# Modulation weights streamed under attention, interleaved projection, and 34 expert units for 35 in a two-layer hybrid block

## The chip, the cores and the metric

One core of one Trainium2 chip. The metric is the device time of the whole program in microseconds (us), the median of several runs; everything is in float32. The core has a matrix engine (TensorE, PE in the rows; PEld is its weight load), VectorE (DVE), ScalarE (ACT), GpSimd (POOL) and an engine that issues DMA transfers (SP). Each engine runs its own program in order and waits for the others by semaphores.

## The reference

Two layers of a hybrid block over 384 tokens of width 1024: tokens 0 to 127 are context (tile t = 0, condition c_ctx), tokens 128 to 383 are samples (tiles 1 and 2, condition c). Each layer computes

```
sh1, sc1, g1, sh2, sc2, g2 = split(cond @ w_mod + b_mod, 6)          # w_mod 1024 x 6144
h = rms_norm(x, g_pre_mix) * (1 + sc1) + sh1
u = h @ w_in                                                         # 1024 x 2816
y_a = silu(layer_norm(dwconv31(u_a1 * sigmoid(u_a2))))               # 256 columns
y_b = hyena(dwconv3(u_b))            # two long convolutions by spectra, gates x1, x2
y_c = rms_norm((softmax(q1 k1) - lam * softmax(q2 k2)) @ v)          # 4 heads; samples also see 128 cached keys
x = x + g1 * rms_norm(concat(y_a, y_b, y_c) @ w_out, g_post_mix)
h = rms_norm(x, g_pre_ffn) * (1 + sc2) + sh2
s = sigmoid(h @ router_w); 4 of 8 groups, then 8 of 64 experts per token
y = swiglu(h, shared) + sum over the 8 experts of weight * swiglu(h, expert e)   # width 256
x = x + g2 * rms_norm(y, g_post_ffn)
```

The outputs are x after both layers and the new keys and values of the context tokens.

## The kernel before

**Weights.** All big weights stream from DRAM by SP's DMAs. The mixer's go through RING, three slots of 4096 columns: per layer 20 chunks (`chunk`, lines 347 to 367) in a fixed order, twelve of w_mod (2 MB each), three and three of w_in, two of w_out; chunk i goes into slot i mod 3 once the chunk three places earlier has been used. The experts use four buffers (two in RING, two in WB); `free` holds a load back until the buffer's owner has been multiplied.

**Mixer, layer by layer, one stage after the other.** Modulation: `mod_chunk` (L552) multiplies a chunk with the two conditions, 16 matmuls; two chunks make a section (one of sh1, sc1, ...), whose row is turned into columns by `mod_columns` (L536). All six sections of a layer are made ahead of everything else, and in between lie the Hyena filters (L847) and their spectra (L570, L574). `gate_rows` (L584, evicted by `grow`, L1034) spreads the gates g1 and g2 over partitions, and `to_features` (L600) transposes the normalised tokens to HT. The projection runs 19 tiles u (L873 feature-major for the conformer and Hyena parts, L883 token-major for q, k, v). Then come the layer norm and the Hyena turns (z transposes, spectra and convolutions, L918 to L943) and the q and k transposes; then attention, 12 units (tile, head) in a software pipeline of 14 iterations (scores L957, transposes L967, values L979, output turns L987); then the output projection w_out (L997) for all three tiles, residual (L1271, L1273), squares (L1045), normalising, transposes, router (L1010), token rows for the gathers (L1017).

**Experts.** Experts are sorted by their token count, and each rank in that order has a fixed width. `parts(u)` makes units: pairs (96 + 32 or 64 + 64 tokens) and single experts of 128. 35 units run in the order WIDE. A unit is one `step` of TensorE: gate and up matmuls (L617) with the next unit's gathered rows transposed in between (L659), the token list of the unit three later (`lists`, L644 or L647: three float32 matmuls of three or two columns), the scatter of the unit before (L671, L672), a flip (L633) and the down matmuls (L626). POOL gathers the token rows and makes the scatter matrices. Tokens beyond a rank's width go to a loop over all 64 experts (`turns`), whose number of rounds is computed on the chip.

Of the kernel before, what the change touches and what calls it, by code (L numbers as in the profile page):

```python
# [47 lines left out]
NCH = NMOD + 3 + 3 + 2  # L48
# [4 lines left out]
NPAIR, NFULL = 29, 6  # L53
NU = NPAIR + NFULL
LSTN, SORTN = 4, 8
# [46 lines left out]
def build(nc, I, O):  # L102
    lam_init = [0.8 - 0.6 * math.exp(-0.3 * l) for l in range(DEPTH)]
    with ExitStack() as ctx:
# [18 lines left out]
        MODC = sb("MODC", [P, 6, KD, 2])  # L123
        ASC = sb("ASC", [P, 2, KD, 2])
# [4 lines left out]
        RSM = sb("RSM", [P, 200])  # L129
        NRD = sb("NRD", [P, DEPTH], mybir.dt.int32)  # L130
        h_rows = nc.dram_tensor("h_rows", [TOK, DM], F32, kind="Internal").ap()
        PASSED = sb("PASSED", [1, 32])

        with ExitStack() as mx:
# [7 lines left out]
            KS = sb("KS", [P, NT, 2, 2, 256], c=mx)  # L142
# [3 lines left out]
            YS = sb("YS", [P, NT, 2, 256], c=mx)  # L146
            ON = sb("ON", [P, 2, P], c=mx)

        with ExitStack() as me:
# [11 lines left out]
            ONEHOT = sb("ONEHOT", [P, 2, NT, P], c=me)  # L161
# [7 lines left out]
            WS = sb("WS", [P, NT, NU, 3], c=me)  # L169
# [28 lines left out]
        PS = [ctx.enter_context(nc.psum_tensor(f"PS{i}", [P, 512], F32)) for i in range(8)]  # L198
# [12 lines left out]

        FLT = QKV[:, :, :].rearrange("p a b -> p (a b)")
# [10 lines left out]
        MROW = HTF[:, 0:2048].rearrange("p (b n) -> p b n", b=2)  # L223
# [5 lines left out]
        M2 = RWF[:, 1280:1792].rearrange("p (a n) -> p a n", a=2)  # L229

        RP = YT[:, 4:8, :].rearrange("p a b -> p (a b)")
        XN = YT[:, :, :].rearrange("p a b -> p (a b)").rearrange("p (t d) -> p t d", t=NT)
        XNK = XN.rearrange("p t (q k) -> p t k q", k=KD)
# [13 lines left out]
        WIDE = (29, 30) + tuple(range(0, 5)) + (31,) + tuple(range(10, 16)) + (32,) + tuple(range(5, 10)) + (33,) + tuple(  # L247
            range(16, 22)) + (34,) + tuple(range(22, 29))
# [23 lines left out]
        chunk_in = [sem(f"chunk_in{i}") for i in range(SLOTS)]  # L272
# [23 lines left out]
        def turns(eng, l):  # L296

            rounds = eng.value_load(NRD[0:1, l:l + 1], min_val=0, max_val=NT)
            if l == 0:
# [9 lines left out]
         a_yss, a_rt, a_tk) = map(sem, (  # L309
             "a_hid", "a_mod", "a_spec", "a_cond", "a_lam", "a_grow", "a_ss", "a_hT", "a_u", "a_zt", "a_ln", "a_qk",  # L310
             "a_exp", "a_PT", "a_oss", "a_OT", "a_yss", "a_rt", "a_tk"))
# [10 lines left out]
        K_FILT, K_MOD, K_AU, K_DU, K_CV, K_SC, K_ROPE, K_LN, K_ZS, K_GATE, K_P = (  # L322
            12, 7, 23, 4, 64, 36, 48, 12, 24, 8, 48)

        def chunk_no(l, i):

            return len(range(i % SLOTS, NCH, SLOTS)) * l + i // SLOTS + 1

        def au(n):

            return {1: 1, 3: 2}[n] if n < 4 else 2 + 2 * (n - 3) if n < 10 else 14 + n - 9
# [14 lines left out]
        def _(sp):  # L346
# [37 lines left out]
            for l in range(DEPTH):  # L384
# [10 lines left out]
                for i in range(SLOTS, NCH):  # L395
                    chunk(l, i)
# [1386 lines left out]
```

## Time and profile before

| | us |
|---|---|
| three runs | 1999.53, 1992.54, 1999.26 |
| median | 1999.26 |
| the profiled execution | 2000.44 |
| its span in the trace | 1998.4 |
| TensorE busy (8604 matmuls) | 1814.4, 91% |
| VectorE, ScalarE, GpSimd busy | 634.9, 377.1, 186.1 |
| DMA | 542.05 MB, mean 271 GB/s |
| mean granted TensorE clock | 0.938 |

Times in the rows are counted from the span's start. The span lies inside the execution; 2.0 us are around it. Layer 0 fills the first half of the span, layer 1 the second. A busy share is an average over stages with different limits, so the rows of the stages say more than this table. The granted clock is a share of full speed (1.0 is 2.4 GHz, 0.5 is 1.2 GHz).

### The profile page before, as it was taken

What the parts mean: (1) busy time and instruction counts of PE and PEld (TensorE: products, weight loads), DVE (VectorE), ACT (ScalarE), POOL (GpSimd) and SP (SyncE); (2) the same over time, 40 slices, a digit from 0 to 9 for tenths busy, and PEclk for the clock granted to TensorE, in tenths of its full rate; (3) what the DMA queues carried; (4) which work ended last, traced back from release to release, by engine and by line L of the source; (5) the groups of instructions that cost most, each with busy time, mean ns of one, the idle gap of its engine ahead of it and who ended that gap; (6) DMA issues with size and microseconds to landing.
All of it is one profiled execution on the core that took longest, in us unless ns stands there. A gap on an engine that the chain in (4) does not pass through costs nothing. (4 is left out here: it accounts for less than half of the span.)

```text
span 1998.4 us, 22439 instructions
## 1 busy us (share of the span) xinstructions
PE 1814.4 (91%) x8604; PEld 896.5 (45%) x8604; DVE 634.9 (32%) x1719; ACT 377.1 (19%) x832; POOL 186.1 (9%) x181
## 2 busy tenths in 40 slices
PE   5899768689999999999888996687899999999995
PEld 1454544544444444444335545335444444444442
DVE  2255461512222222222241835605122222222222
ACT  2210241301111111111222102403111111111111
POOL 0000000011111111111000000100111111111110
PEclk8899968899999999999969998698899999999998
DMA  9723000287999999999584320002789999999992
GB/s 404 321 85 126 11 1 0 95 328 295 415 392 418 393 411 390 419 393 415 232 359 189 127 95 0 1 28 82 321 343 414 392 419 393 404 399 416 395 416 112
DMA packets 77435, 542.05 MB, mean 271 GB/s; under 512 B 8336, under 2 KB 11408, under 8 KB 21776
## 3 DMA queue, kind: packets, MB, share of 16 engines
q1 hardware_dynamic: 67248, 503.90, 61.8%
q0 software_dynamic: 10080, 36.70, 4.6%
q8 instruction: 70, 1.15, 0.2%
q14 instruction: 37, 0.30, 0.0%
HBM read 534.80 MB, written 5.77 MB: 270 GB/s over the span
## 5 line engine op out<-in xcount | busy, mean ns | idle before, releaser
L617 PE MATMUL PS<-RING,EX 128*32 128x512 f32 (+2 forms) x1280 | 387.3, 598 | 1.7 <-DVE EX L1424 1.7
L617 PE MATMUL PS<-WB,EX 128*32 128x512 f32 (+2 forms) x1408 | 387.5, 598 | 0.0
L626 PE MATMUL PS<-RING,AT 128*32 128x512 f32 (+2 forms) x688 | 220.5, 611 | 4.3 <-ACT AT L1077 3.2
L1442 DVE TENSOR_TENSOR YL<-PS,YH 128x512 fp32r<-128x512 f32 x140 | 96.9, 692 | 368.8 <-ACT YH L1093 347.2
L626 PE MATMUL PS<-WB,AT 128*32 128x512 f32 (+2 forms) x704 | 189.0, 596 | 0.0
L671 PE MATMUL PS<-YH,SCAT 128*128 128x512 f32 x420 | 177.2, 422 | 2.9 <-DVE YL L1442 2.9
L466 POOL TENSOR_SCALAR SCAT<-CST,LSTT 128x384 fp32r<-128x384 f32 x70 | 87.7, 1252 | 897.0 <-PE PS L672 885.9
L617 PEld LDWEIGHTS PS<-WB,EX 128*32 128x32 f32 (+2 forms) x1408 | 103.0, 126 | 144.1 <-issue 144.1
L672 PE MATMUL PS<-YL,SCAT 128*128 128x512 f32 x420 | 166.1, 395 | 0.0
L617 PEld LDWEIGHTS PS<-RING,EX 128*32 128x32 f32 (+2 forms) x1280 | 102.8, 128 | 119.0 <-issue 119.0
L1424 DVE COPY EX<-PS 128x512 f32<-128x512 f32 x70 | 48.4, 692 | 329.1 <-PE PS L659 329.1
L1093 ACT ACTIVATE YH<-PS 128x512 fp32r<-128x512 f32 x140 | 83.7, 598 | 249.0 <-PE PS L626 249.0
L883 PE MATMUL PS<-RING,HT 128*128 128x512 f32 x288 | 123.9, 592 | 0.0
L659 PEld LDWEIGHTS PS<-CST,XG 128*128 128x128 f32 x560 | 61.7, 142 | 107.9 <-issue 107.9
L873 PE MATMUL PS<-HT,RING 128*128 128x384 f32 x320 | 103.7, 486 | 1.5 <-ACT HT L1051 1.5
L626 PEld LDWEIGHTS PS<-RING,AT 128*32 128x32 f32 (+2 forms) x688 | 64.2, 138 | 80.1 <-issue 78.4
L552 PE MATMUL PS<-RING,COND 128*32 128x512 f32 x384 | 60.0, 754 | 36.0 <-DMA RING<-in_wmod 32.6
L659 PE MATMUL PS<-CST,XG 128*128 128x128 f32 x560 | 91.2, 286 | 0.0
L452 POOL TENSOR_TENSOR ST<-ST,HALF 128x1 f32<-128x1 f32 (+1 forms) x32 | 20.0, 624 | 754.0 <-DVE ST L1645 499.2
L671 PEld LDWEIGHTS PS<-YH,SCAT 128*128 128x128 f32 x420 | 79.8, 190 | 21.7 <-issue 4.9
L997 PE MATMUL PS<-RING,YT 128*128 128x512 f32 x192 | 86.8, 615 | 0.9 <-ACT YT L1217 0.9
L626 PEld LDWEIGHTS PS<-WB,AT 128*32 128x32 f32 (+2 forms) x704 | 53.1, 126 | 76.7 <-issue 76.2
(250 smaller groups left out, 1872.6 us busy)
## 6 DMA issues: line engine op xcount, KB each, us to landing
RING<-in_exp_w_gate SPq DMA_DIRECT2D x64, 1024.0 KB
RING<-in_exp_w_up SPq DMA_DIRECT2D x64, 1024.0 KB
RING<-in_exp_w_down SPq DMA_DIRECT2D x64, 1024.0 KB, 12.1
WB<-in_exp_w_gate SPq DMA_DIRECT2D x64, 1024.0 KB
WB<-in_exp_w_up SPq DMA_DIRECT2D x64, 1024.0 KB
WB<-in_exp_w_down SPq DMA_DIRECT2D x64, 1024.0 KB, 12.0
RING<-in_wmod SPq DMA_DIRECT2D x24, 2048.0 KB, 12.6
RING<-in_wtm SPq DMA_DIRECT2D x6, 2048.0 KB, 7.7
```

The source lines that it names most:

```text
L466: nc.gpsimd.tensor_scalar(SCAT[:, s % 2, :], cst("iota"), LSTT[:, s:s + 1], None, ALU.is_equal).then_inc(p_scat, 1)
L552: mm = nc.tensor.matmul(PS[6 + hf][MT * c:MT * (c + 1), :], COND[:, 4 * part + c, :], w[:, c, hf * 512:(hf + 1) * 512], start=(part == 0), ...
L617: mm = nc.tensor.matmul(PS[6][s0:s0 + w, :].rearrange("p (w f) -> p w f", w=2), e[:, k, s0:s0 + w], rawgu[n % NBUF][:, k], start=(k == 0), ...
L626: mm = nc.tensor.matmul(dst[s0:s0 + w, :], AT[:, j, s0:s0 + w], rawdn[n % NBUF][:, hf, j], start=(j == 0), stop=(j == 1))
L659: mm = nc.tensor.transpose(PS[7][:, c * P:(c + 1) * P], XG[:, s % 2, k * P:(k + 1) * P], ident)
L671: nc.tensor.matmul(PS[piece][:, :], w, YHb[s % 2][:, cols], start=False, stop=False, skip_group_check=True)
L672: mm = nc.tensor.matmul(PS[piece][:, :], w, YLb[s % 2][:, cols], start=False, stop=True, skip_group_check=True)
L873: mm = nc.tensor.matmul(PS[n % 6][:, 0:TOK], w[:, k, :], HT[:, k, :], start=(k == 0), stop=(k == KD - 1))
L883: mm = nc.tensor.matmul(PS[n % 6][:, :], HT[:, k, t * P:(t + 1) * P], w[:, k, :], start=(k == 0), stop=(k == KD - 1))
L997: mm = nc.tensor.matmul(PS[2 * t + hf][:, :], YT[:, f, t * P:(t + 1) * P], w[:, f, :], start=(f == 0), stop=(f == 7))
L1093: sc.activation(YHb[s % 2][:, hf * 512:(hf + 1) * 512], PS[6 + hf][:, :], ACT.Copy).then_inc(a_yh, 1)
L1442: v.tensor_tensor(YLb[s % 2][:, hf * 512:(hf + 1) * 512], PS[6 + hf][:, :], YHb[s % 2][:, hf * 512:(hf + 1) * 512].bitcast(F32), ALU.subtr ...
```

## The change

It does five things.

- **Modulation is streamed.** The 24 chunks of both layers have numbers 0 to 23. Chunks 0 to 3 (sh1, sc1 of layer 0) stay in front; 4 to 15 (the rest of layer 0, and sh1, sc1 of layer 1) are loaded and multiplied inside layer 0's attention, one per iteration, 16 to 23 inside layer 1's. They use RING's slot 0 and a fourth slot, KSYS, in which the filter spectra lie earlier in the layer. Some pieces of tile 0's output projection go between the attention units too.
- **The projection is interleaved.** The 19 tiles u run in another order, and the filters, their spectra, the Hyena turns, the layer norm's means and the q and k transposes stand between them in TensorE's program.
- **Residual, squares, normalising and transposes go by tile** behind the output projection (and behind the experts), and each power on POOL is of one tile. The first shared-expert matmul stands ahead of the last router tile, the gate rows of g2 in the list stage.
- **34 units for 35**: eleven 96+32, nineteen 64+64, four 128, in another order.
- **The lists are float32r**: the one-hot matrix and the values are of that type, each value in two columns (a high and a low part), six or four columns.

The diff, cut to its core:

```diff
-NPAIR, NFULL = 29, 6
+NPAIR, NFULL = 30, 4
-LSTN, SORTN = 4, 8
+LSTN, SORTN = 4, 10
...
-            KS = sb("KS", [P, NT, 2, 2, 256], c=mx)
+            KSYS = sb("KSYS", [P, NT * 1536], c=mx)
...
-            ONEHOT = sb("ONEHOT", [P, 2, NT, P], c=me)
+            ONEHOT = sb("ONEHOT", [P, 2, NT, P], F32R, c=me)
-            WS = sb("WS", [P, NT, NU, 3], c=me)
+            WS = sb("WS", [P, NT, NU, 6], F32R, c=me)
...
+        chunk = [RING[:, a * CHW:(a + 1) * CHW] for a in range(SLOTS)] + [KSYS[:, 0:CHW]]
...
-            if u < 10:
+            if u < 11:
                 return ((2 * u, 96, ((0, 32), (32, 32), (64, 32))), (2 * u + 1, 32, ((96, 32),)))
...
-        WIDE = (29, 30) + tuple(range(0, 5)) + (31,) + tuple(range(10, 16)) + (32,) + tuple(range(5, 10)) + (33,) + tuple(
-            range(16, 22)) + (34,) + tuple(range(22, 29))
+        WIDE = (30, 31) + tuple(range(0, 6)) + (32,) + tuple(range(11, 18)) + (33,) + tuple(range(6, 11)) + tuple(range(18, 30))
...
+        ORDER = (4, 5, 6, 7, 8, 9, 0, 1, 2, 3) + tuple(range(10, 19))
+        def fill(l, i):
+
+            first, n = (4, 12) if l == 0 else (16, 8)
+            return first + i if i < n else None, (first + i) // 2 - 1 if 0 < i <= n and i % 2 == 0 else None
+
+        def pieces(l, i):
+
+            if l == 0:
+                return range(0, 2) if i == 12 else range(2, 4) if i == 13 else range(0)
+            return range(i - 9, i - 8) if 9 <= i < 12 else range(3, 5) if i == 12 else range(5, 7) if i == 13 else range(0)
...
@@ block.sync @@
+            def mod_in(j):
+
+                if j == 3:
+                    sp.wait_ge(mod_used, 2)
+                elif j > 5 and j not in (16, 17):
+                    sp.wait_ge(mod_used, j - 1)
+                a = SLOT_OF["m", j][0]
+                sp.dma_start(chunk[a], I["wmod"][j // NMOD, j % NMOD]).then_inc(chunk_in[a], 16)
...
+                tiles_done(l, 13)
+                mod_in(fill(l, 0)[0])
+                tiles_done(l, 16)
+                weight_in(l, "o0")
+                sp.wait_ge(pe_conv, 4 * (l + 1))
+                mod_in(fill(l, 1)[0])
+                tiles_done(l, 19)
+                weight_in(l, "o1")
...
+                for i in range(2, NUN):
+                    if fill(l, i)[0] is not None:
+                        mod_in(fill(l, i)[0])
+                sp.wait_ge(mod_used, 15 if l == 0 else 23)
                 sp.dma_start(raw[0][:, 0:2048], I["sh_w_gate"][l].rearrange("(p k) n -> p (k n)", p=P)).then_inc(gu_in[0], 16)
...
@@ block.tensor, lists @@
-                        mm = nc.tensor.matmul(PS[7][:, 256:259], ONEHOT[:, s % 2, t, :], WS[:, t, u, :],
+                        mm = nc.tensor.matmul(PS[7][:, 256:262], ONEHOT[:, s % 2, t, :], WS[:, t, u, :],
...
@@ block.tensor, the layer @@
+                for i in range(19):
+                    u_tile(l, i)
+                    if l > 0 and i < 2:
+                        hidden(l, i)
+                    if 2 <= i < 5:
+                        filters(l, i - 2)
+                    if 5 <= i < 8:
+                        spectra(l, i - 5)
+                    if i in (8, 13):
+                        z_turn(l, i // 10)
+                    if i in (9, 14):
+                        z_spectra(l, i // 10)
+                    if i in (11, 16):
+                        z_conv(l, (i - 10) // 5)
+                    if i >= 16 and i < 18:
+                        conv_mean(l, i - 16)
+                    if i >= 17:
+                        for h in range(NH):
+                            qk_turn(l, i - 17, h)
...
+                        if i >= 1:
+                            pe.wait_ge(a_exp, 2 * (NUN * l + i))
                         for c in range(2):
-                            mm = nc.tensor.matmul(PS[2 * (i % 2) + c][:, 0:kn * P],
+                            mm = nc.tensor.matmul(PS[c][:, 0:kn * P],
...
+                    j, sec = fill(l, i)
+                    if sec is not None:
+                        mod_columns(sec)
+                    if j is not None:
+                        mod_chunk(j)
+                    for p in pieces(l, i):
+                        w_out_piece(l, p)
                     if 1 <= i <= NUN:
                         pe.wait_ge(a_PT, NUN * l + u + 1)
...
+                gate_rows(l, 0, 0)
+                for p in range(4 if l == 0 else 7, 8):
+                    w_out_piece(l, p)
+                gate_rows(l, 0, 1)
+                pe.wait_ge(a_OT, NUN * (l + 1))
+                w_out(l, 1, 0)
+                w_out(l, 1, 1)
+                to_features(l, 1, 0)
+                pe.wait_ge(a_grow, 8 * l + 4)
+                w_out(l, 2, 0)
+                to_tokens(l, 0)
+                w_out(l, 2, 1)
+                to_features(l, 1, 1)
+                router(l, 0)
+                to_tokens(l, 1)
+                router(l, 1)
+                shared_up(l, 0)
+                to_features(l, 1, 2)
+                router(l, 2)
+                to_tokens(l, 2)
+                mixture_pe(l)
...
@@ block.gpsimd @@
-                own.sig(nc.gpsimd.tensor_tensor(ST[:, a + w:a + 2 * w], ST[:, a:a + w], HALF[:, 0:w], ALU.pow), p_pow)
+                own.sig(nc.gpsimd.tensor_tensor(ST[:, a + w:a + w + 1], ST[:, a:a + 1], HALF[:, 0:1], ALU.pow), p_pow)
```

## Rows read from the trace of the kernel before

**Rows 1.** The page's slices: busy tenths in 40 equal parts of the span.
```profile
PE   5899768689999999999888996687899999999995
DMA  9723000287999999999584320002789999999992
```

**Rows 2.** Stages: window, length, PE, PEld, DVE, ACT, POOL busy, granted clock, DMA share, GB/s.
```profile
14.80:83.40 68.60, 56.27 (x324) 23.01 (x324) 16.47 (x37) 17.14 (x29) 0.85 (x1) 0.90 1.01 427
100.30:214.00 113.70, 113.61 (x304) 57.62 (x304) 58.29 (x152) 10.44 (x24) 0.00 (x0) 1.00 0.26 97
214.00:254.20 40.20, 28.77 (x132) 22.98 (x132) 24.80 (x44) 11.04 (x23) 0.00 (x0) 0.92 0.00 0
254.20:311.30 57.10, 36.79 (x144) 21.03 (x144) 33.65 (x108) 25.76 (x96) 6.53 (x12) 0.64 0.00 1
311.30:352.00 40.70, 40.66 (x91) 18.04 (x92) 0.00 (x0) 3.45 (x10) 0.00 (x0) 0.96 0.00 0
437.20:989.10 551.90, 548.36 (x2972) 251.35 (x2972) 135.21 (x365) 89.22 (x174) 76.46 (x67) 1.00 0.92 378
989.10:1072.30 83.20, 67.66 (x327) 27.59 (x325) 27.52 (x49) 21.34 (x41) 4.54 (x4) 0.75 0.88 350
1243.60:1301.20 57.60, 37.14 (x139) 21.17 (x138) 33.62 (x108) 25.84 (x96) 6.53 (x12) 0.65 0.00 1
```

**Rows 3.** Timeline: start us, length us, engine, line; between the layers and in layer 1.
```profile
1004.43 0.69 DVE L1273 TENSOR_TENSOR X<-X,SCR 128x512 f32<-128x512 f32 x1
1087.76 1.53 PE L873 MATMUL PS<-HT,RING 128*128 128x384 f32 x4 [0.78 <-ACT HT L1051]
...
1300.49 1.22 PE L997 MATMUL PS<-RING,YT 128*128 128x512 f32 x1 [0.46 <-ACT YT L1217]
1355.45 1.06 ACT L1045 ACTIVATE SCR<-X 128x1024 f32<-128x1024 f32 x1 [10.62 <-issue]
1376.55 0.33 ACT L1230 ACTIVATE SCR<-PS 128x192 f32<-128x192 f32 x1 [4.47 <-PE PS L1010]
1427.15 2.81 PE L617 MATMUL PS<-RING,EX 128*128 128x512 f32 x6 [0.87 <-DVE EX L1424]
```

**Rows 4.** Chain of waits in layer 1's experts: start us, length us, what.
```profile
1537.46 2.77 PE PS L617 x6
1552.53 2.73 PE PS L617 x12
...
1600.18 2.60 PE PS L617 x12
1616.01 2.60 PE PS L617 x12
1624.38 0.76 PE PS L644 x6
```

**Rows 5.** Two pairs in the middle of a run of pairs, columns as in rows 2.
```profile
626.90:642.70 15.80, 15.80 (x80) 7.09 (x78) 3.93 (x12) 2.57 (x5) 2.28 (x2) 1.00 1.02 421
642.70:658.50 15.80, 15.80 (x76) 7.16 (x73) 3.94 (x12) 2.56 (x5) 2.28 (x2) 1.00 1.01 412
```

**Rows 6.** Timeline of TensorE in the first modulation stage.
```profile
30.85 3.64 PE L552 MATMUL PS<-RING,COND 128*32 128x512 f32 x16 [3.55 <-DMA RING<-in_wmod]
37.34 1.92 PE L552 MATMUL PS<-RING,COND 128*32 128x512 f32 x16
44.09 1.95 PE L536 MATMUL PS<-FOLD,HT 128*128 128x2 f32 x16
```

**Rows 7.** Groups by line: busy us, mean ns of one, idle time before.
```profile
L574 PE MATMUL PS<-QKV,CST 128*128 128x512 f32 x32 | 14.8, 604 | 0.0
L847 PE MATMUL PS<-PR,CO 64*128 64x512 f32 x24 | 14.5, 729 | 0.9 <-ACT CO L1134 0.9
L570 PE MATMUL PS<-QKV,CST 128*128 128x512 f32 x8 | 5.7, 854 | 0.0
```

**Rows 8.** DMA issues of the page: KB each, median us from issue to landing.
```profile
RING<-in_exp_w_down SPq DMA_DIRECT2D x64, 1024.0 KB, 12.1
RING<-in_wmod SPq DMA_DIRECT2D x24, 2048.0 KB, 12.6
```

More of the change, by code:

```diff
@@ L551, in mod_chunk @@
+            def mod_chunk(j):
+                a, n = SLOT_OF["m", j]
+                part = j % 2
+                if j == 0:
+                    pe.wait_ge(d_cond, 3)
+                pe.wait_ge(chunk_in[a], 16 * n)
+                w = chunk[a].rearrange("p (c n) -> p c n", c=4)
+                for hf in (1, 0):
                     for c in range(4):
@@ L569, in spectra @@
                         w = cst("cf1" if part == 0 else "sf1")
-                        mm = nc.tensor.matmul(PS[b + part][:, :], w, f[:, 0, :], start=True, stop=True)
+                        mm = nc.tensor.matmul(PS[1 + part][:, :], w, f[:, 0, :], start=True, stop=True)
                     else:
@@ new lines, in router @@
+            def router(l, t):
+                features_done(l, 1, t)
+                if t == 0:
+                    pe.wait_ge(a_tk, 6 * l + 2)
+                rw = par("rw").rearrange("p (k e) -> p k e", k=KD)
+                for k in range(KD):
+                    mm = nc.tensor.matmul(PS[7][:, t * NE:(t + 1) * NE], HT[:, k, t * P:(t + 1) * P], rw[:, k, :],
+                                          start=(k == 0), stop=(k == KD - 1))
+                if t == NT - 1:
+                    mm.then_inc(pe_rt, 1)
@@ new lines, in w_out @@
+            def w_out(l, t, hf, first=0, last=8):
+                if first == 0:
+                    a, count = SLOT_OF[l, f"o{hf}"]
+                    pe.wait_ge(chunk_in[a], 16 * count)
+                w = chunk[SLOT_OF[l, f"o{hf}"][0]].rearrange("p (f n) -> p f n", f=8)
+                for f in range(first, last):
+                    mm = nc.tensor.matmul(PS[YB[0][t] + hf][:, :], YT[:, f, t * P:(t + 1) * P], w[:, f, :],
+                                          start=(f == 0), stop=(f == 7))
+                if last == 8:
+                    mm.then_inc(pe_y, 1)
@@ L1184, in _ @@
-                z_out(0)
+                act.wait_ge(p_pad, 2 * (l + 1))
+                for i in range(19):
+                    u_out(l, i)
+                    if l > 0 and i < 2:
+                        hidden(l, i)
+                    if 5 <= i < 8:
+                        spectra(l, i - 5)
+                    if i in (8, 13):
+                        z_out(l, i // 10)
+                    if i >= 17:
+                        for h in range(NH):
+                            qk_out(l, i - 17, h)
@@ L1516, in _ @@
[L1516 to L1524 removed]
+                dve.wait_ge(pe_filt, NT * l + t + 1)
@@ L1526, in _, with gated, taps @@
+            def gated(l, c):
+                dve.wait_ge(pe_u, 19 * l + PLACE[2 * c] + 1)
+                dve.wait_ge(a_u, K_AU * l + au(2 * c + 1))
+                ps = PS[3 + PLACE[2 * c] % 3]
+                sig(v.tensor_tensor(CB[:, c, CPAD:CPAD + P], ps[:, 0:P], SG[:, c, 0:P], ALU.mult), d_u)
+                sig(v.tensor_tensor(CB[:, c, 2 * CPAD + P:2 * CPAD + TOK], ps[:, P:TOK], SG[:, c, P:TOK], ALU.mult), d_u)
+            def taps(first, last):
                 cw = par("cw").rearrange("p (c w) -> p c w", c=2)
-                for w in range(CW):
+                for w in range(first, last):
```

1177 lines of the change are left out of this document (645 added, 532 removed).

## Prediction, made before the result was known

> **What bounds the kernel now.** First the page's slices: the DMA engines are near full in two kinds of stretch, the expert stages (slices 9 to 19 and 29 to 39) and the modulation stages (slices 1, 2 and 20, 21), and nearly idle between them [rows 1]. Then the table by stages [rows 2], in microseconds from the span's start. Layer 0 streams twelve modulation chunks to 83.4 at 427 GB/s, so that stage is set by DMA. It projects from 100.3 to 214.0 with TensorE busy 113.6 of 113.7 and DMA at 97 GB/s. The Hyena and layer-norm part follows to 254.2 (TensorE 28.8 of 40.2, VectorE 24.8), attention to 311.3 (TensorE 36.8 of 57.1, at a mean granted clock of 0.64), the output projection to 352.0. Routing and the shared expert end at 437.2, and the experts run to 989.1 with TensorE busy 548 of 552. So the kernel alternates: where DMA is full TensorE has slack, where TensorE is full DMA is free, and attention fills neither. Layer 1 repeats it: 98.7 us pass between its predecessor's last scatter (989.1) and its first projection at 1087.8 [rows 2, 3].
>
> Inside the expert stage the chain of waits is TensorE alone: a 64+64 unit goes from 1600.18 to 1616.01, 15.83 us, a full unit from 1537.46 to 1552.53, 15.07 [rows 4]. DMA is only just behind: in a run of pairs its share is 1.01 to 1.02 at 412 to 421 GB/s [rows 5]. A pair needs 6.29 MB of weights and 0.52 MB of gathered rows, 6.81 MB, 16.2 to 16.5 us at those rates: already more than 15.83. The full units (3.67 MB, 8.9 us) pay that back.
>
> **The change, part by part.** All is summed against the profiled span, 1998.4, with 2.0 around it (2000.4; the median of the runs is 1999.3, 1.1 lower).
>
> (A) Front of layer 0. Only chunks 0 to 3 stay ahead of the first projection; gate rows and the other eight chunks leave. Before, chunk 2 began at 30.85, chunk 3 ended at 39.3 and the columns of its section at 46.0 [rows 6]. The same chunks arrive in the same queue order, chunk 3 one wait later, so I keep 46, add one us of VectorE scaling and 6 for transposes and evictions of three tiles: projection at 53 instead of 100.3, **-47**. The projection weights are issued behind chunk 3 and land by about 51, an estimate.
>
> (B, G) Projection with Hyena folded in. TensorE's work is summed: 113.6 + 28.8 [rows 2] + filters and spectra, which leave the modulation stage and were half of 14.5 + 5.7 + 14.8 = 17.5 [rows 7], together 160. Before, the stretch lasted 153.9. VectorE's work, 58.3 + 24.8 [rows 2] and some 8 for filters, is 91 of 160 and, traced through the order by hand, early at each place where TensorE waits for it; if one such wait opens, each us of it is a us of span. **+6** in layer 0, **+7** in layer 1, which has two filter matmuls more. Bounds: -4 (small matmuls overlap better between tiles) to +20 (taps late at one turn).
>
> (C, H) Attention with the streamed chunks. Its own work is 36.8 x 0.64 = 23.5 us at full clock [rows 2]. Twelve chunks at 1.92, six column sets at 1.95 [rows 6] and four output pieces at 1.7 (a twenty-fourth of 40.7 [rows 2] each) add 41.6: 65.1 at 2.4 GHz, 130 at 1.2 GHz, where a chunk takes 3.64 [rows 6]. Which clock? Attention got 0.64 and 0.65; the modulation stages, the same chunks and columns, 0.90 and 0.75 [rows 2]. I take 0.75: 87, plus 5 because the first four iterations (128 keys) are shorter than a chunk's transfer, 2.1 MB at 427 GB/s, 4.9 us. 92 for 57.1: **+35**. Layer 1 has eight chunks, four column sets, seven pieces: (24 + 35)/0.75 + 2 = 81 for 57.5: **+23**. Bounds 70 to 135 and 61 to 121. Two added waits stand here. Scores now use one pair of banks, so TensorE waits for both exponentials of the unit before, with all its later work queued behind; the chunk in between covers that. And a chunk's arrival holds back value products and the next scores. SP issues chunk j when chunk j-2 is used, two iterations (13 us) ahead; in the full queue a chunk took 12.6 from issue to landing [rows 8], less when alone. Behind these issues in SP's queue stand the shared weights, an estimated 60 us before use.
>
> (D, I) From the output projection to the first expert. In layer 1 it lasts 76 (1300.5 to the router's sigmoid at 1376.55) and 50.6 more to 1427.15 [rows 3]; layer 0 is the same to a us. Before, all tiles wait for the last projection, then residual, squares, normalising and transposes follow with TensorE idle. Now each tile does so under the next tile's projection. TensorE's sum: gate rows 6, the rest of the projection 33.8 (40.7 - 6.9), transposes and router of tiles 0 and 1 10, the first shared matmul 7, the last tile's transposes, evictions, router and sigmoid 6.5: 63, **-13**; layer 1, with three pieces more in attention, 58, **-18**. After the sigmoid the first shared matmul (7) and two thirds of the token transposes are gone and 6 of gate rows come in: **-3** each. POOL's powers become one per tile, each under its tile's chain, and its zero fills move behind them; no gather is passed. Bounds for the whole: -5 to -30 per layer.
>
> (E, J) Experts. Thirty pairs and four full units for 29 and six: 30 x 15.83 + 4 x 15.07 = 535.2 for 549.5, -14.3. The lists are six matmul records in 0.76 us on the chain [rows 4]; single pass makes it three: -0.38 x 34 = -12.6 (bounds 0, if a float32r load with six columns costs double, to -17, if also the wait before the transposes shrinks). A pair's TensorE step is then 15.45, further under DMA's 16.2 to 16.5. The cover is the lead: downs land 12.1 after issue [rows 8], which is at the end of a unit; the gates and ups queued ahead of them land 5 earlier, some 8.7 before their unit begins. At a deficit of 0.9 a run of six or seven pairs lives on that; the new last run of 17 needs 15 and stalls some 6. **-21** per layer (bounds -10, at 412 GB/s throughout and no lead left over, to -31).
>
> A row and a rule differ here. The Trainium skill (DMA: Bandwidth & Descriptors, "Where 436 GB/s comes from") gives 435 GB/s as the fabric's ceiling and says that for HBM loads a lower limit of about 358 binds. The trace's 412 to 421 [rows 5] is above the lower one; by 358 a pair would take 19.0 us (an estimate by that page), by 435 it takes 15.7, still above 15.45. So the rule speaks against this part of the change, and its outcome is the second rival.
>
> (F) Between the layers. The twelve chunks and gate rows of layer 1 are gone; weights of the first projection are issued after the last scatter and land, by estimate, within 20 us, beside the residual. The adds ended at 1005.1 [rows 3]. The last tile then needs squares (1.06 [rows 3]), power, scaling, eight transposes and four evictions: 8.5, an estimate. Projection at 1013.6 instead of 1087.8: **-74**.
>
> Sum: -47 + 6 + 35 - 16 - 21 - 74 + 7 + 23 - 21 - 21 = -129: 1998.4 - 129 + 2.0 = 1871.4, and 1870 against the median. Removed in all is about 200; attention and projection take 71 back.
>
> **The rivals.** (1) Attention at 2.4 GHz, TensorE never waiting long enough to lose the clock: 70 and 61, 42 less: 1828. For it: the first modulation stage was granted 0.90 with TensorE busy 56 of 69. Against: the second got 0.75 with TensorE busy 68 of 83 [rows 2]. (2) DMA sets every pair: 30 x 16.4 + 4 x 14.7 = 551, nothing gained from the experts: 1912. For it: a share of 1.0 already. Against: no wait of TensorE for weights in the expert stage of before. (3) Attention wholly at 1.2 GHz: 135 and 121, 83 more: 1953. For it: 0.64 and 0.65 granted in attention before, with TensorE idle a third of the time [rows 2]. Against: it will hardly idle. (4) Nothing measurable: every chunk shows its whole 12.6 [rows 8], 20 x 12.6 + 8 other iterations of 4.4 (57.1/13 [rows 2]), 287 in place of the forecast's 173: +114, 1984. Against: two are in flight. (5) Slower, by one place: the slots. Each rank of expert gets a fixed width; rank 3 falls from 128 to 96, rank 15 from 128 to 64, rank 53 from 64 to 32. One token too many at one rank and the leftover loop runs over all 64 experts, one after the other, each waiting for its own weights: 64 x (12.1 + 15.1) = 1740 more, 3610. It decides from one token on. Counted from the reference's router on its own inputs, those ranks hold 87, 62 and 28 tokens in layer 0 and 90, 63 and 30 in layer 1: the tightest has one to spare, and rounding on the chip would have to move two. (6) The lists stay at two passes: +26, 1896, inside the range.
>
> **How the numbers follow.** Forecast (with 6) 0.60, (1) 0.17, (2) 0.12, (3) 0.06, (4) 0.03, (5) 0.02. The forecast's own bounds are about 1835 to 1910; the range takes in (1) with a little more from the lists, and (2) and part of (3): 1815 to 1935. A measurement of this kernel tells about 0.5%, 10 us, from no change: faster 0.95, same 0.03, slower 0.02.
>
> **What would show it.** First projection near 53 in layer 0, and some 25 after the last scatter in layer 1. Attention: 92 and 81, with a granted clock near 0.75; a clock of 0.95 is rival 1, 0.5 rival 3, TensorE waiting for RING in it rival 4. Pair units of 15.45 with list records at three; TensorE waiting for weights only late in the last run; 16.4 from the start is rival 2. Wrong altogether if projection with Hyena shows TensorE waiting for VectorE over 20 us, or if the tile chain after the output projection leaves TensorE idle as before.

## The result and the profile after

The changed kernel takes **1822.46 us** (median of four runs, 1816.30 to 1823.92) against 1997.55 for the kernel before on the same chips (four runs): a ratio of 0.9121, 95% interval 0.9093 to 0.9149. The forecast was 1870 with a range of 1815 to 1935, so the sign and the range held; the gain is 175 us where 129 were forecast. The time lies below the forecast's own bounds (about 1835 to 1910): the range holds it because it was drawn to take in rival 1. The profiled execution has a span of 1822.1, 176.3 less than before.

The page's slices answer to [rows 1]: the DMA engines are no longer full in the modulation stages, because these are gone as stages, and the gaps between the expert stages are shorter.

```profile
PE   4999799989999999999959997999999999999995
DMA  9212581198999999999832137315799999999993
```

The stages by windows answer to [rows 2] (window, length, PE, PEld, DVE, ACT, POOL busy, granted clock, DMA share, GB/s). In order: layer 0's projection with the Hyena turns inside it, attention with twelve chunks, output projection to first expert (the tail, below), experts, the stretch between the layers; then layer 1's projection, attention, tail and experts.

```profile
50.09:204.50 154.41, 153.01 (x468) 83.98 (x469) 83.25 (x178) 20.47 (x49) 0.00 (x0) 1.00 0.23 85
204.50:290.70 86.20, 72.71 (x449) 36.01 (x450) 36.99 (x121) 37.22 (x119) 6.58 (x12) 0.84 0.77 293
290.70:392.40 101.70, 95.09 (x381) 55.07 (x379) 33.93 (x128) 28.42 (x55) 6.78 (x10) 0.95 0.31 120
392.40:919.40 527.00, 522.64 (x2899) 230.72 (x2899) 131.92 (x358) 86.45 (x169) 74.12 (x65) 1.00 0.96 401
919.40:944.80 25.40, 5.94 (x26) 4.76 (x25) 18.62 (x38) 12.91 (x31) 6.06 (x8) 0.60 0.57 227
944.80:1103.00 158.20, 156.79 (x472) 85.14 (x473) 88.05 (x190) 22.68 (x52) 0.00 (x0) 0.99 0.23 83
1103.00:1177.65 74.65, 60.84 (x364) 31.50 (x365) 37.00 (x121) 35.18 (x113) 6.58 (x12) 0.91 0.60 226
1177.65:1276.50 98.85, 91.80 (x368) 54.34 (x367) 33.92 (x128) 28.41 (x55) 6.56 (x9) 0.93 0.32 124
1276.50:1803.50 527.00, 521.97 (x2896) 230.28 (x2897) 131.95 (x358) 86.45 (x169) 74.11 (x65) 1.00 0.96 399
```

With the same marks in both traces (first matmul of a stage; last scatter) the ledger of the forecast reads, in us of the span:

| term | before | after | measured | forecast |
|---|---|---|---|---|
| A, front of layer 0 | 100.3 | 50.1 | -50.2 | -47 |
| B, projection, layer 0 | 153.9 | 154.4 | +0.5 | +6 |
| C, attention, layer 0 | 57.1 | 86.2 | +29.1 | +35 |
| D, to the first expert | 125.9 | 101.7 | -24.2 | -16 |
| E, experts | 551.9 | 526.9 | -25.0 | -21 |
| F, between the layers | 98.7 | 25.5 | -73.2 | -74 |
| G, projection, layer 1 | 155.2 | 158.2 | +3.0 | +7 |
| H, attention, layer 1 | 57.5 | 74.6 | +17.1 | +23 |
| I, to the first expert | 126.7 | 98.9 | -27.8 | -21 |
| J, experts | 552.0 | 527.5 | -24.5 | -21 |
| end of the span | 19.3 | 18.1 | -1.2 | 0 |

The sum is -176.4 against -129. No term has the wrong sign; nine of the ten are a few us better than forecast, and together they make the 47 us that are missing.

### The profile page after: what moved, and what is told of

Same layout as the page of the kernel before. It is cut to its first block, busy times and chain, and to the rows that moved or that the text cites. A ratio compares the mean times of both kernels' runs of the same rounds, so it can differ in the third digit from the quotient of the medians.

```text
span 1822.1 us, 22136 instructions
## 1 busy us (share of the span) xinstructions
PE 1705.8 (94%) x8440; PEld 824.3 (45%) x8440; DVE 617.4 (34%) x1669; ACT 377.0 (21%) x850; POOL 187.2 (10%) x193
## 4 chain that ended last, share of the span: by engine, by line
PE 87%; DMA 6%; DVE 3%; ACT 2%; issue 1%; SPq 0%; ACTq 0%; POOL 0%; DVEq 0%
PE PSB L836 29%; PE PSB L845 14%; PE PSB L828 7%; PE PSB L823 6%; PE PSB L890 5%; PE PSB L891 5%; PE PSB L791 4%; PE PSB L878 4%; PE PSB L626 2%; DMA RING<-in_wmod 2%; PE PSB L863 1%; DMA X<-in_x 1%; DMA WB<-in_exp_w_up 1%; DMA RING<-in_exp_w_up 1%; DMA KSYS<-in_wmod 1%; PE PSB L852 1%
## 5 line engine op out<-in xcount | busy, mean ns | idle before, releaser
L836 PE MATMUL PSB<-WB,EX 128*32 128x512 f32 (+2 forms) x1408 | 432.1, 598 | 0.2 <-DMA RING<-in_exp_w_up 0.2
L836 PE MATMUL PSB<-RING,EX 128*32 128x512 f32 (+2 forms) x1344 | 417.3, 598 | 3.8 <-DMA WB<-in_exp_w_up 2.1
L845 PE MATMUL PSB<-RING,AT 128*32 128x512 f32 (+2 forms) x720 | 229.8, 602 | 4.9 <-issue 3.8
L845 PE MATMUL PSB<-WB,AT 128*32 128x512 f32 (+2 forms) x704 | 210.8, 596 | 0.0
L890 PE MATMUL PSB<-YH,SCAT 128*128 128x512 f32 x408 | 172.1, 422 | 2.8 <-DVE YL L1647 2.8
L836 PEld LDWEIGHTS PSB<-WB,EX 128*32 128x32 f32 (+2 forms) x1408 | 113.1, 126 | 136.0 <-issue 136.0
L836 PEld LDWEIGHTS PSB<-RING,EX 128*32 128x32 f32 (+2 forms) x1344 | 105.8, 124 | 124.8 <-issue 124.8
L891 PE MATMUL PSB<-YL,SCAT 128*128 128x512 f32 x408 | 161.2, 395 | 0.0
L828 PE MATMUL PSB<-RING,HT 128*128 128x512 f32 x288 | 125.6, 592 | 0.0
L823 PE MATMUL PSB<-HT,RING 128*128 128x384 f32 x320 | 109.0, 495 | 3.3 <-ACT HT L1191 3.3
```

The costliest lines, as they stand in the source:

```text
L823: mm = nc.tensor.matmul(PS[3 + i % 3][:, 0:TOK], w[:, k, :], HT[:, k, :], start=(k == 0), stop=(k == KD - 1))
L828: mm = nc.tensor.matmul(PS[3 + i % 3][:, :], HT[:, k, t * P:(t + 1) * P], w[:, k, :], start=(k == 0), stop=(k == KD - 1))
L836: mm = nc.tensor.matmul(PS[6][s0:s0 + w, :].rearrange("p (w f) -> p w f", w=2), e[:, k, s0:s0 + w], rawgu[n % NBUF][:, k], start=(k == 0), ...
L845: mm = nc.tensor.matmul(dst[s0:s0 + w, :], AT[:, j, s0:s0 + w], rawdn[n % NBUF][:, hf, j], start=(j == 0), stop=(j == 1))
L890: nc.tensor.matmul(PS[piece][:, :], w, YHb[s % 2][:, cols], start=False, stop=False, skip_group_check=True)
L891: mm = nc.tensor.matmul(PS[piece][:, :], w, YLb[s % 2][:, cols], start=False, stop=True, skip_group_check=True)
```

## The experiments

Each kernel is the changed one with one edit (the better version has two; the three that leave chunks or their work out also hold the loop for tokens over the width at zero rounds). Stage lengths are read with the same marks as above. First, how well such a reading repeats: the changed kernel itself was run once more.

> The changed kernel itself, beside the others on the same chip. Theory 1, the stages repeat within 2 us except attention, whose clock differs from execution to execution (81.7 to 86.2 and 74.6 to 77.5 in the runs with the same attention so far): time 1822. Theory 2, the chip of this job differs as a whole: all stages move by the same share.

1819.63 us (six runs, 1815.96 to 1824.06), ratio 0.9117 (0.9092 to 0.9143). Theory 1 holds for most stages: projection 155.9 and 159.4, experts 528.4 and 529.3. The tail, 98.9 and 95.7, is some 3 us shorter. Layer 0's attention is 82.5 at a granted clock of 0.92 in place of 86.2 at 0.84, layer 1's 74.1:

```profile
206.60:289.00 82.40, 67.62 (x448) 34.45 (x449) 36.98 (x121) 37.86 (x119) 6.58 (x12) 0.92 0.80 307
1101.20:1175.30 74.10, 61.14 (x364) 30.97 (x365) 37.00 (x121) 35.15 (x113) 6.57 (x12) 0.91 0.60 227
```

In the runs whose experts have the changed kernel's code and order, they take 526.7 to 531.3. So in a single profile a difference of under 5 us in attention, the tail or the experts means nothing.

**Thirty-four units for thirty-five.**

```diff
-NPAIR, NFULL = 30, 4
+NPAIR, NFULL = 29, 6
-            if u < 11:
+            if u < 10:
...
+        WIDE = (29, 30) + tuple(range(0, 5)) + (31,) + tuple(range(10, 16)) + (32,) + tuple(range(5, 10)) + (33,) + tuple(
+            range(16, 22)) + (34,) + tuple(range(22, 29))
```

> The changed kernel with the 35 units (29 pairs, six full) and the order of units of the kernel before; all else stays. Theory 1, TensorE sets each unit: a pair takes 15.50 us and a full unit 14.73 in the changed kernel, so a layer takes 29 x 15.50 + 6 x 14.73 = 537.9 for 30 x 15.50 + 4 x 14.73 = 523.9, +14.0 per layer; the expert stage 541 for 527.0, the time about 1850. Theory 2, DMA sets the expert stage (6.81 MB of a pair at 426 GB/s are 16.0 us, a full unit's 3.67 MB 8.6): the bytes are nearly the same, so the stage stays near 527 and the time near 1822.

1850.75 us (ratio 0.9266, 0.9224 to 0.9307); the expert stages take 541.0 and 541.2. This is theory 1, which asked for 541 (that it agrees to a tenth is luck, as the stage repeats within 5 us only): TensorE sets the units, and exchanging two full units for one pair is worth 10 to 14 us per layer, although the bytes hardly change.

**The lists in one pass.** Before, a list was six matmul records with 0.69 us from its start to the first scatter (timeline of the kernel before, start us, length us, line):

```profile
634.41 0.83 PE L644 MATMUL PS<-WS,ONEHOT 128*128 128x3 f32 x6
635.10 0.47 PE L671 MATMUL PS<-YH,SCAT 128*128 128x512 f32 x1
```

After, it is three records and 0.35 us, with six columns in place of three:

```profile
568.53 0.50 PE L863 MATMUL PSB<-WS,ONEHOT 128*128 128x6 f32 x3
568.88 0.48 PE L890 MATMUL PSB<-YH,SCAT 128*128 128x512 f32 x1
```

```diff
-mm = nc.tensor.matmul(PS[7][:, 256:262], ONEHOT[:, s % 2, t, :], WS[:, t, u, :],
+mm = nc.tensor.matmul(PS[7][:, 256:262], ONEHOT[:, s % 2, t, :].bitcast(F32), WS[:, t, u, :].bitcast(F32),
...
```

> The changed kernel with its list matmuls read as float32 (two passes) in place of float32r, the same six columns; all else stays. Theory 1, each list stands in TensorE's path: 0.34 us more per unit (0.69 from list to scatter before, 0.35 now), 34 x 0.34 = +11.6 per layer, expert stage 538.6, time about 1845. Theory 2, DMA sets the pairs at 16.0 us already: a pair at 15.84 still fits under it, less than +4 per layer, time at most 1830.

1841.42 us (0.9220, 0.9178 to 0.9262), expert stages 537.6 and 536.1: +10.7 and +8.6 of the 11.6 per layer. Theory 1: each list stands in TensorE's path. With pairs of 15.84 no wait for weights is left in either layer, so the 0.8 and 1.5 us of it that the changed kernel has (below) are to be taken off the 11.6.

**The order of the units.**

```diff
-        WIDE = (30, 31) + tuple(range(0, 6)) + (32,) + tuple(range(11, 18)) + (33,) + tuple(range(6, 11)) + tuple(range(18, 30))
+        WIDE = (30, 31, 32, 33) + tuple(range(0, 6)) + tuple(range(11, 18)) + tuple(range(6, 11)) + tuple(range(18, 30))
```

> The changed kernel with all four full units in front and then the thirty pairs in one run; the same units, bytes and matmuls. Theory 1, the forecast's lead: TensorE wants a pair in 15.50 us, DMA brings one in 16.0 (6.81 MB at 426 GB/s), so 30 pairs run up 15 us against a lead of about 9: TensorE waits some 6 us for weights late in each run, expert stage 533, time about 1834. Theory 2, the DMA engines can do more than 426 GB/s when asked: no wait, stage 527, time 1822.

1838.08 us (0.9207, 0.9165 to 0.9249), expert stages 536.4 and 533.8. TensorE's waits for DMA in layer 0's expert stage, first of the changed kernel, then of this one (engine, tile, line, what it waited for: us in total, times, longest):

```profile
PE PSB L836 <- DMA WB<-in_exp_w_up: 0.6, 1, 0.6
PE PSB L836 <- DMA RING<-in_exp_w_up: 0.2, 1, 0.2
```

```profile
PE PSB L836 <- DMA WB<-in_exp_w_up: 4.8, 8, 1.0
PE PSB L836 <- DMA RING<-in_exp_w_up: 1.9, 7, 0.3
```

6.7 us in layer 0 and 6.3 in layer 1, in fifteen and fourteen short waits: theory 1, the 6 us of the forecast's lead. In layer 0 the run of pairs begins at 447.4 and the first wait comes at 665.5, after 14 pairs; from there on nearly each pair waits, 0.45 us in the mean. DMA moved 426 GB/s at a share of 1.01 for 200 us on end:

```profile
700.00:900.00 200.00, 194.90 (x994) 83.89 (x991) 47.20 (x127) 31.70 (x62) 26.27 (x23) 1.00 1.01 426
```

So a pair costs 15.50 on TensorE and 16.0 on DMA, and the four full units in between are what makes the first of these the time.

**The start of attention.** TensorE's first long wait in the changed attention is one that the forecast put at nothing: the scores use one pair of banks now, so those of the second unit wait for the first unit's exponentials, and the chunk in between does not cover this, because the exponentials come late. ScalarE's timeline there: square root, sigmoid and exponential each load their table (1.28 us), and VectorE's reciprocal and products lie in between.

```profile
204.43 1.28 ACT L1372 ACT_TABLE_LOAD   x1
205.73 0.52 ACT L1372 ACTIVATE SG<-SG 128x384 f32<-128x384 f32 x1
206.27 1.28 ACT L1375 ACT_TABLE_LOAD   x1
210.91 0.94 ACT L1375 ACTIVATE SG<-CB 128x384 f32<-128x384 f32 x2 [3.35 <-DVE CB L1884]
211.86 1.28 ACT L1389 ACT_TABLE_LOAD   x1
213.60 0.37 ACT L1389 ACTIVATE HT<-PSB,ST 128x128 f32<-128x128 f32 x1 [0.46 <-DVE ST L1920]
```

```diff
                         for h in range(NH):
                             qk_out(l, i - 17, h)
+                    if i == 17:
+                        act.wait_ge(d_ln, K_LN * l + 5)
+                        own.sig(sc.activation(SG[:, 0, :], SG[:, 1, :], ACT.Sqrt), a_ln)

-                act.wait_ge(d_ln, K_LN * l + 5)
-                own.sig(sc.activation(SG[:, 0, :], SG[:, 1, :], ACT.Sqrt), a_ln)
```

> The changed kernel with the layer norm's square root on ScalarE (and its table load) moved ahead of the last projection tile's eviction, where ScalarE is idle for 6.4 us; all else stays. Theory 1, the 7.6 us in which TensorE waits at the start of attention for the first exponential are the chain square root, reciprocal (2.55), sigmoid, three table loads of 1.28: some 5 us of it go per layer, attention 81 and 69.5 for 86.2 and 74.6, time about 1812. Theory 2, the chunks' arrival sets attention: the wait moves from the exponential to the chunks, at most 2 us per layer, time 1819 or more.

1811.21 us (0.9071, 0.9027 to 0.9114); attention 79.5 and 73.4. The waits of layer 0's attention, changed kernel and this one:

```profile
PE PSB L1100 <- ACT HT L1389: 7.6, 1, 7.6
PE PSB L626 <- DMA RING<-in_wmod: 3.9, 2, 2.6
PE PSB L626 <- DMA KSYS<-in_wmod: 1.7, 2, 1.1
```

```profile
PE PSB L626 <- DMA KSYS<-in_wmod: 4.8, 4, 2.0
PE PSB L626 <- DMA RING<-in_wmod: 3.8, 2, 2.5
PE PSB L1100 <- ACT HT L1390: 2.4, 1, 2.4
```

Both theories have a part. The wait for the exponential falls by 5.2 as theory 1 said; the waits for chunks are 8.6, for 5.6 in the changed kernel and 7.1 in its repetition, as theory 2 said. Layer 0's stage gains 3 to 7 us; in layer 1 it gains 1, which is within the spread.

**What the chunks cost.** Two runs take the transfers away, wholly or to a quarter, and a third the matmuls too.

```diff
+                w = CHW if j < 4 else CHW // 4
-                sp.dma_start(chunk[a], I["wmod"][j // NMOD, j % NMOD]).then_inc(chunk_in[a], 16)
+                sp.dma_start(chunk[a][:, 0:w], I["wmod"][j // NMOD, j % NMOD][:, 0:w]).then_inc(chunk_in[a], 16)
...
```

> The changed kernel with only the first quarter (0.5 MB of 2 MB) of each of the chunks 4 to 23 transferred; the matmuls on them stay, on what the slot held, so the modulation behind sh1 and sc1 of layer 0 is not the reference's, and the loop for tokens over the width is held at zero rounds. Theory 1, TensorE's lowered clock in attention (0.84 and 0.91 granted) comes from its waits, for chunks among them (5.6 and 4.9 us): these waits go, the clock rises, attention is near its sum at full clock plus the 7.6 at its start, about 71 and 64 for 86.2 and 74.6, time about 1797. Theory 2, the clock is lowered by attention's own gaps: only the waits go, 81 and 70, time about 1812.

1807.43 us (0.9063, 0.9041 to 0.9086); attention 74.4 at a clock of 0.91 and 70.1 at 0.90:

```profile
205.80:280.20 74.40, 66.17 (x448) 34.27 (x449) 36.95 (x121) 36.77 (x119) 6.58 (x12) 0.91 0.39 129
1094.20:1164.30 70.10, 61.20 (x364) 31.22 (x365) 36.94 (x121) 34.74 (x113) 6.59 (x12) 0.90 0.31 106
```

All waits for chunks are gone. Layer 1 falls by 4 us, no more than its waits of 4.9, at an unchanged clock: theory 2. Layer 0 falls by 12 from the first profile (waits of 5.6, a clock of 0.84) and by 8 from the repetition (waits of 7.1, a clock of 0.92). Against the repetition this is theory 2 within a us; against the first profile the gain lies between the theories.

```diff
-                    for c in range(4):
+                    for c in range(4 if j < 4 else 1):
                         mm = nc.tensor.matmul(PS[6 + hf][MT * c:MT * (c + 1), :], COND[:, 4 * part + c, :],
...
```

> The changed kernel without the transfers of chunks 4 to 23 and with two of each chunk's sixteen matmuls (on a constant tile); column sets, gate rows and output pieces stay; the modulation behind sh1 and sc1 of layer 0 is left out so, and the loop for tokens over the width is held at zero rounds. Theory 1, a chunk in attention costs about what its matmuls take (1.92): attention falls to about 60 in either layer (86.2 and 74.6 with chunks; 57.1 and 57.5 before, without column sets and pieces), at a clock as low as before (0.65), time about 1780. Theory 2, attention is set by the chain of exponential and VectorE, and the chunks fill idle time: at least 76 and 68, time 1805 or more.

1807.23 us (0.9066, 0.9050 to 0.9083); attention 77.6 and 68.3. By these numbers theory 2 would stand, but the trace shows that the edit did not take TensorE's work away. A chunk of the changed kernel, and one of this run with a quarter of its matmuls:

```profile
204.94 1.93 PE L626 MATMUL PSB<-RING,COND 128*32 128x512 f32 x16
```

```profile
205.15 1.90 PE L627 MATMUL PSB<-CST,COND 128*32 128x512 f32 x4
```

A chunk is eight float32 matmuls, each of them two records, and two of the eight are left here. Sixteen records take 1.93 and four take 1.90: the four matmuls that write 32 partitions each run side by side. The Trainium skill (TensorE: Matmul & The Clock Gate, Part 3: Packing small matmuls) says that small matmuls with tile positions of their own run concurrently in the same array, and the run agrees. So this run measured the transfers alone, once more, and was repeated with the matmuls cut in columns:

```diff
+                        n = 512 if j < 4 else 16
...
-                                              w[:, c, hf * 512:(hf + 1) * 512], start=(part == 0), stop=(part == 1))
+                                              w[:, c, hf * 512:hf * 512 + n], start=(part == 0), stop=(part == 1))
...
```

> The run without chunks once more, with each chunk's two remaining matmuls cut from 512 to 16 columns: in the run before they took 1.90 us, as long as the chunk's sixteen records did, so TensorE's work had not gone. Transfers and matmuls of chunks 4 to 23 are left out, the loop for tokens over the width is held at zero rounds. Theory 1, chunk matmuls stand in attention's path: 12 x 1.9 and 8 x 1.9 go from the 77.6 and 68.3 of the run before, and some of that comes back by a lower clock: about 60 and 57, time about 1780. Theory 2, an iteration is set by exponential and VectorE (57.1 / 13 = 4.4 before) once it is free of chunks: 13 x 4.4 and pieces and start, at least 70 and 65, time 1800 or more.

1809.72 us (0.9070, 0.9039 to 0.9101), and attention takes 77.4 and 75.8: not less than with the chunks' matmuls. The windows of the two attention stages in the run before and in this one:

```profile
204.70:282.30 77.60, 69.36 (x305) 35.01 (x306) 36.96 (x121) 36.75 (x119) 6.59 (x12) 0.87 0.16 56
1096.60:1164.90 68.30, 59.36 (x269) 30.24 (x270) 36.95 (x121) 34.70 (x113) 6.59 (x12) 0.93 0.18 63
```

```profile
204.40:281.80 77.40, 64.69 (x304) 44.23 (x305) 36.96 (x121) 36.45 (x119) 6.57 (x12) 0.63 0.16 55
1092.90:1168.70 75.80, 63.46 (x268) 42.72 (x269) 36.99 (x121) 34.55 (x113) 6.57 (x12) 0.64 0.16 57
```

A unit's scores over 384 keys, in this run and, with the chunks' matmuls in place, in the better version below:

```profile
252.29 1.65 PE L1102 MATMUL PSB<-KT,QT 64*128 64x384 f32 x4
```

```profile
249.37 0.92 PE L1103 MATMUL PSB<-KT,QT 64*128 64x384 f32 x4
```

Theory 2's time is met, but theory 2's chain is the smaller part of it. In layer 0 the chunks' matmuls fall from 25.7 us to 4.4, yet TensorE's busy time falls by 4.7 only, and its idle time grows by 4.5: it waits 9.2 us for the first exponentials where it waited 7.6, and 3.1 for VectorE in five places where it did not wait. The rest is the clock. It is 0.63 and 0.64 here, as in attention before [rows 2], and the other matmuls take so much longer that the stage's length stays or grows. So in this attention a chunk's matmuls cost no time on balance; what costs is its arrival, 4 to 12 us per layer by the two runs without waits for chunks.

Without chunks attention still takes 77.4 and 75.8 for 57.1 and 57.5 before. Column sets, output pieces and the wait at the start are in it; no run takes these apart.

**The token tiles.**

```diff
                 w_out(l, 1, 1)
-                to_features(l, 1, 0)
                 pe.wait_ge(a_grow, 8 * l + 4)
                 w_out(l, 2, 0)
+                w_out(l, 2, 1)
+                pe.wait_ge(d_xn, 6 * l + 6)
+                to_features(l, 1, 0)
                 to_tokens(l, 0)
-                w_out(l, 2, 1)
                 to_features(l, 1, 1)
...
```

(VectorE's, ScalarE's and POOL's steps are regrouped in the same way.)

> The changed kernel with the three token tiles kept together behind the output projection: all projections first, then squares, residual, normalising of all tiles, then the transposes; gate rows, powers by tile and the early shared matmul stay as changed. Theory 1, the forecast's: what the change gains from the output projection to the first expert (24 and 28 us) is mostly the chain of squares, power, residual and normalising hidden under the next tile's projection: some 12 us per layer come back, tail 114 and 111 for 101.7 and 98.9, time about 1846. Theory 2, the gain is from the moved gate rows and token transposes: at most 4 us per layer, time at most 1830.

1861.77 us (0.9335, 0.9311 to 0.9359); the tails take 119.2 and 114.9, +17 and +16. One wait of TensorE for the normalised tokens makes most of it:

```profile
344.88 1.97 PE L756 MATMUL PSB<-CST,QKV 128*128 128x128 f32 x8 [14.88 <-DVE QKV L1450]
```

Theory 1, and more than it asked for: of the 24 and 28 us that the change gains here, some two thirds are this chain hidden by tile. The rest was not taken apart by a run. From the chain of waits in the changed kernel's tail (start us, length us, what), the router of tiles 0 and 1, then the gate rows of g2 in the list stage:

```profile
331.39 1.73 PE PSB L779 x16
334.08 1.73 PE PSB L779 x16
374.08 1.89 PE PSB L743 x16
381.37 1.79 PE PSB L743 x16
```

**The interleaved projection.**

```diff
                 for i in range(19):
                     u_tile(l, i)
...
+                for o in range(2):
+                    z_turn(l, o)
+                    z_spectra(l, o)
+                    z_conv(l, o)
+                    conv_mean(l, o)
+                for c in range(2):
+                    for h in range(NH):
+                        qk_turn(l, c, h)
...
```

(ScalarE's and VectorE's steps are moved along.)

> The changed kernel with the Hyena turns, the layer norm's means and the q and k transposes behind all nineteen projection tiles again (filters and their spectra stay in between); on VectorE all taps and rotations stand ahead of the Hyena products. Theory 1, interleaving fills the gaps of the Hyena stage, which before took 40.2 us with TensorE busy 28.8: some 12 us per layer come back, projection 166 and 170 for 154.4 and 158.2, time about 1846. Theory 2, VectorE, not TensorE, sets this stretch in either order: at most 3 us per layer, time at most 1829.

1856.62 us (0.9309, 0.9282 to 0.9337), projection 171.2 and 177.0.

> The run with the Hyena turns behind the projection once more, with the layer norm's first mean behind the second turn (in the run before it was written where the second turn's spectra overwrote it, so its values were not the reference's). The order is else the same, so every theory wants the same times: projection 171 and 177 and a time near 1857 if the values played no part, as the instructions and waits are the same; another time would mean that the earlier one hung on its values.

1854.80 us (0.9288, 0.9254 to 0.9322), projection 172.6 and 173.9: +18 and +16, the values played no part, and theory 1 holds with half as much again. The waits of layer 0's stretch in this run:

```profile
PE PSB L704 <- DVE KSYS L1791: 6.2, 2, 3.2
PE PSB L721 <- DVE SG L1870: 2.2, 1, 2.2
PE PSB L690 <- ACT RW L1300: 1.9, 2, 1.0
PE PSB L823 <- ACT HT L1189: 1.5, 1, 1.5
PE PSB L678 <- DVE CO L1801: 1.3, 1, 1.3
```

The projection hides 11.6 us of such waits (all but the fourth row, which lies ahead of the first matmul, in the changed kernel too), and the rest is slower matmuls: TensorE is busy 159.6 for 153.0 with the same work. The Hyena stage of the kernel before had three of these waits, of 6.3, 1.9 and 1.3 us, so they are not peculiar to this run's order on VectorE.

**A better version.** The early root and a third slot for chunks:

```diff
-            [("m", 1), ("m", 3), (0, "f0"), (0, "t2"), (0, "o1"), (1, "f0"), (1, "t2"), (1, "o1")],
+            [("m", 1), ("m", 3), (0, "f0"), (0, "t2"), ("m", 6), ("m", 9), (0, "o1"),
+             (1, "f0"), (1, "t2"), ("m", 18), ("m", 21), (1, "o1")],
...
                 tiles_done(l, 19)
-                weight_in(l, "o1")
+                mod_in(fill(l, 2)[0])
...
+                sp.wait_ge(mod_used, 10 if l == 0 else 22)
+                weight_in(l, "o1")
```

> The changed kernel with the early square root and with a third slot for chunks: 6, 9, 18 and 21 go into RING's slot 1 behind the last q, k, v weights, and that slot's half of the output projection is loaded after them. Theory 1, attention waits for chunks because only two are in flight: the waits for chunks (5.6 and 4.9) and 5 of the 7.6 at the start go, attention about 74 and 66 for 86.2 and 74.6, time about 1802. Theory 2, the transfers themselves are the limit (2.1 MB at 427 GB/s are 4.9 us, twelve are 59 of 86): three in flight share the same rate, the waits for chunks stay, time about 1811 as with the early root alone.

**1798.93 us** (six runs, 1793.97 to 1803.68), ratio 0.9015 (0.8990 to 0.9040), beside 1819.63 and 0.9117 for the changed kernel on the same chip. Attention takes 70.4 and 63.4:

```profile
206.60:277.00 70.40, 64.02 (x449) 33.81 (x450) 32.52 (x117) 35.48 (x117) 6.59 (x12) 0.98 0.90 359
1091.10:1154.50 63.40, 59.33 (x364) 30.96 (x365) 32.53 (x116) 33.10 (x111) 6.59 (x12) 0.95 0.65 266
```

Theory 1: layer 1 waits for no chunk any more, layer 0 for 3.5 us at a DMA share of 0.90 in the window, so the transfers are now nearly its limit. TensorE idles 6.4 and 4.1 us in these stages, and the clock is granted at 0.98 and 0.95; in the run with quarter chunks it idled 8.2 and 8.9, at 0.91 and 0.90. The two edits were not measured apart beyond the run with the early root alone.

## Why the prediction was right, and where it was short

- **Direction, and the large terms (A, F).** The alternation of full DMA and full TensorE was the right reading: taking the modulation stages away gave 50.2 and 73.2 where 47 and 74 were forecast. Between the layers 25.5 us are left, in which TensorE is busy 5.9 [the fifth window above]. Of the 47 us by which the whole came out better, the tail has 15, attention 12, projection 9.5, experts 7.5 and the front 3.
- **Attention (C, H), +46 for +58.** Two terms were mis-sized, and they partly cancel. One is the clock: 0.75 was taken; 0.84 and 0.91 were granted, 0.92 and 0.91 in the repetition. TensorE was busy 72.7 where 87 was forecast. Against this stands the wait for the first exponentials, put at nothing: 7.6 us per layer at the start, for the table loads and the layer norm's tail, where 5 were allowed for all waits in layer 0 and 2 in layer 1; they come to 13.5 and 13.8. Before, this chain lay inside the separate Hyena stage, next to other work. So rival 1's direction was right, and its 70 and 61 are nearly what the better version reaches (70.4 and 63.4), with most of the waits gone. That the whole kernel landed near rival 1's 1828 is chance: its attention did not happen, and three quarters of the 47 us lie elsewhere. The forecast's reason for the price, that a chunk costs its matmuls' time, did not hold: the run without them is no faster.
- **The tail (D, I), -52 for -37.** The mechanism was right (the tiles' chains under the next tile's projection, 16 to 17 us by the run that undoes it). The sum to the sigmoid was 6 and 4 too large (56.8 and 53.7 for 63 and 58): transposes and router of tiles 0 and 1 take 7.0 for the 10 put down, gate rows 3.9 for 6, and the last tile's part in layer 0 4.9 for 6.5. Behind the sigmoid 45 pass for the 47.6 forecast: the gate rows of g2 stand on the chain there, with 3.7 for the 6 put down.
- **Projection (B, G), +3.5 for +13.** The sum added the Hyena stage's 28.8 as it stood, at a granted clock of 0.92 [rows 2], and half the filters and spectra from a stage at 0.90. Inside the projection all of it runs at 1.0: TensorE is busy 153.0 for the 160 of the sum. VectorE was indeed early everywhere: TensorE idles 1.4 us in layer 0's stretch, and none of it is a wait for VectorE.
- **Experts (E, J), -49.5 for -42.** Units and lists came as summed: 15.50 for a pair where 15.45 was forecast. The stall of 6 us in the run of 17 pairs did not come: 0.8 us in layer 0 and 1.5 in layer 1. The term that was mis-sized is DMA's rate: 412 to 421 GB/s were read from single pairs [rows 5], 425 to 426 are sustained, so the deficit is 0.5 per pair for the 0.9 of the forecast, and the lead covers 14 to 15 pairs: in the run of 17 only the next to last pair and, in layer 0, the last one wait; in the run of 30 nearly all from the fifteenth on do. (0.38 x 34 in the forecast's sum is 12.9, not 12.6; its -21 stays.)
- **The other rivals.** (2), DMA sets every pair, and the Trainium skill's lower limit beside it (DMA: Bandwidth & Descriptors, "Where 436 GB/s comes from"), did not happen: 426 GB/s is far above 358 and near the ceiling of 435 that the same section gives. (3) needed 0.5 in attention; 0.84 was granted. (4) needed every chunk to show its latency; four of layer 0's twelve chunks waited, 5.6 us in all (six and 7.1 in the repetition). (5) did not occur: the loop for leftover tokens left no record in the trace. (6) did not occur either: two passes would have cost 19 to 22 us.

The mis-sized terms of attention's clock, the tail and the projection lean the same way: durations or clocks taken from stages with a low clock were carried over into stages that are dense. The wait at the start of attention leans the other way. What stays open is the attention clock itself: between executions of the same code layer 0's attention was 81.7 to 86.2, and no row here says why the clock fell at one chunk and not at another.

## What to carry to other kernels

Where one stage leaves DMA idle and the next leaves TensorE idle, moving a stream of weights from the second into the first can pay twice: the stream's own stage goes, and, as the run without the chunks' matmuls shows here (0.63 for 0.87), the added work goes with a higher clock for the small matmuls around it. Price such a move by the waits it adds, here the chunks' arrival and a chain of table loads that lost its cover, more than by its matmuls. And when a unit's time on one engine comes within a few per cent of its time on DMA, the order of the units can decide whether the difference is seen, as in the run of thirty pairs.

## What was not expected of the hardware

- Cutting TensorE's work on twelve chunks from 25.7 us to 4.4 in a stage of 78 us left its length unchanged, mainly because the granted clock fell from 0.87 to 0.63; in layer 1 the stage grew from 68.3 to 75.8.
- Four matmuls with outputs on 32 partitions each took as long as one of them (1.93 for sixteen records, 1.90 for four), so an experiment that drops three of the four takes no time away.
- A float32r list with six columns took half the time of a float32 list with three (0.35 for 0.69 from its start to the next matmul).
